# Moving modulation products, convolution steps and the compressed weighing inside the first two layers of a four-engine transformer kernel

## Chip, cores and metric

The kernel runs on one core of one Trainium2 chip, as one program. The metric is device time in microseconds (us), from the first to the last instruction of an execution, as the median of several executions. The engines that matter are PE (TensorE, matmuls), DVE (VectorE), ACT (ScalarE), POOL (GpSimd) and SP (SyncE, which issues the weight loads).

## What is computed

Everything is float32, with 256 tokens of width 1024. Two "first" layers run, and then one "second" block. Cut to what matters:

```python
for l in range(2):                      # the two first layers
    h = rms_norm(x, pre_mix)
    proj = h @ w_in                     # q, kv, gate, conv and pool inputs
    o_a = cmp_attention + selected_attention + window_attention
    o_b = silu(layer_norm(causal_conv31(a * sigmoid(g))))     # 512 channels
    o_c = pool_mixer(...);  o_d = sliding_window_attention(...)
    up = einsum(branches, w_branch);  gates = sigmoid(h @ w_gate)
    x = x + rms_norm(sum(gates * up) @ w_o)
    hf = rms_norm(x, pre_ffn)
    x = x + rms_norm((gelu(gate) * val) @ w_down)   # gate, val: conv3(hf @ w_up)
# second block: it starts from x and from modulation vectors
mods = silu(c) @ w_mod + b_mod          # 6 x 1024, for c and for c_ctx
```

`mods` needs nothing from the first layers. The kernel works it out inside them.

## The kernel before, in words

**Weights.** All weights come in chunks of 128 x 2048 floats (1 MB) through a ring of four slots, `ring`. The chunk with index c of a layer goes to slot c % 4. SP issues the loads strictly in the order of the index, in the loop of line 450, and each load first waits until PE has used the chunk four places ahead of it. A layer has 92 chunks. Most are *split* chunks: ACT rounds the chunk (`split_hi`, L423) into a high part, DVE subtracts (`split_lo`, L428, into `ring_low`), and PE then makes three matmuls for each product. A few chunks are *raw*: PE reads them from the ring. Raw ones are the compression weights, one pad chunk and the modulation halves. The list `layer_chunks()` says which chunk is of which kind, and `SPLIT_CHUNKS[n]` gives the chunk index of split n.

**Modulation.** In each layer there are 6 steps of 512 columns, each in two halves (`mod_half`, L495, one raw chunk, four column groups), then ACT copies the row (`mod_out`), PE turns it (`mod_turn`, L508) and DVE adds the bias (`mod_in`, L1160). Steps 0 to 2 stand among the 16 gate blocks, steps 3 to 5 among the 22 feed-forward blocks.

**Every engine's order is written by hand.** A layer's stages on PE are:

1. `turn_normed("ht")` (L482), then the projections kv, kv2, q, dq, two split chunks each (L547 to L551).
2. Gate inputs, compression, convolution and pool inputs.
3. Seven rounds (r = 0 to 6) of two gate blocks each (L577 to L581), with the attention's scores (L704), the turning of its probabilities (L717) and its values (L734, L740) in between. `cmp_out` turns the compressed probabilities `csc` in round 1. It needs DVE's `cmp_weigh` (L1348 to L1357).
4. Sixteen branch products (`up`, L794 to L798) in the order of branches 2, 0, 3, 1. In front of `up` (0, 3) PE turns the convolution's result `acc` (`convT`, L482), which needs all 124 convolution steps of DVE (`conv_steps`, L1267). Later it turns the normed result (`obT`).
5. The output projection `wo`, four split chunks (L813 to L817), then `turn_normed("hf")` behind two norms, the feed-forward blocks (L835 to L839), and the down projection (L857 to L861).

**DVE in a round:** `mask` twice (wait for PE's scores), `split_lo` for one gate block, `weigh` twice (wait for ACT's exponentials), `split_lo` for the next gate block, then 12 convolution steps. In round 1 `cmp_weigh` comes behind the first `split_lo`.

**ACT behind the output projection.** For each column half c of `wo`, ACT first splits two chunks and then squares the result. For c = 1 these two are the first two chunks of the feed-forward stage (FIRST_WO is 38, FIRST_FFN is 42):

```python
for c in range(2):
    for n in range(FIRST_WO + 2 + 2 * c, FIRST_WO + 4 + 2 * c):
        split_hi(act, n)
    for t in range(TT):
        post_square("wo", c, t)
```

DVE has the same order (`split_lo` of both, then `residual`). At a layer's end ACT calls the next layer's `highs_head` (its splits 0 and 1) and then `post_square("down", 1, t)`; DVE calls `lows_head` and then `residual("down", 7)`. Behind `post_square` come POOL's roots, DVE's residual, and the next norm: ACT's square (L887), POOL's root, DVE's gains (L1141), ACT's scaling (L892), and then PE's `turn_normed`.

Of the kernel before, what the change touches and what calls it, by code (L numbers as in the profile page):

```python
# [27 lines left out]
F32 = mybir.dt.float32  # L28
# [186 lines left out]
def plan_layer(jobs):  # L215
    for t in range(TT):
        for c in range(2):
            jobs.plan(("ht", t, c))
# [40 lines left out]
    for i in range(MOD_STEPS // 2):  # L259
# [18 lines left out]
    for i, r in zip(range(3, MOD_STEPS), ("s0", "s1", "t")):  # L278
# [7 lines left out]
CONV_BEFORE = (0, 3)  # L286
OB_BEFORE = {(3, 1): 0, (3, 2): 1}
# [3 lines left out]
def layer_block(nc, l, mem, ring, ring_low, landed, used, wts, psum, sems, cols_dram, rows_dram, turner_in, placed, wait_x, wait_scratch):  # L291
# [161 lines left out]
    def tensor_program(pe):  # L453
# [32 lines left out]

        def mod_half(i, half):
# [28 lines left out]
        def next_split():  # L516

            n = split_at["n"]
            split_at["n"] += 1
            assert state["chunk"] == SPLIT_CHUNKS[n], (state, n)  # L520
# [11 lines left out]
        pe.wait_ge(turner_in, 16)  # L532
        turn_normed("ht", 1)

        for w in ("kv", "kv2", "q", "dq"):
            for half in range(2):
# [19 lines left out]
                else:  # L556
                    jobs.fill(mm, (w, 1))
                    release(w)

# [264 lines left out]

        turn_normed("hf", 2)
# [47 lines left out]
    def scalar_program(act, next_heads):  # L873
# [178 lines left out]
        for n in range(FIRST_UP + 2, FIRST_UP + 6):  # L1052
            split_hi(act, n)
        for t in range(TT):
            if t == 1:
                split_hi(act, FIRST_UP + 6)
# [8 lines left out]
        for n in range(FIRST_UP + 7, FIRST_WO + 1):  # L1065
# [32 lines left out]
        for j in range(FB + 1):  # L1098
# [13 lines left out]
            if j < FB:  # L1112
                if MOD_AFTER_FFN.get(j - 1, (0, 0))[1] == 1:
                    mod_out(MOD_AFTER_FFN[j - 1][0])
# [14 lines left out]
    def vector_program(dve, next_heads):  # L1129
# [74 lines left out]
        for t in range(TT):  # L1204
            jobs.wait_drained(dve, ("kv", t))
            dve.tensor_copy(kd[:, t, :, :, :], bc(proj[:, t, 0:256].rearrange("p (m d) -> p m d", m=4).unsqueeze(2), [P, 4, 2, DH]))\
               .then_inc(kd_ready, 1)
        split_lo(dve, 4)
# [160 lines left out]
        for r in range(len(ROUNDS) + 1):  # L1369
# [9 lines left out]
            if r == 1:  # L1379
                cmp_weigh()  # L1380
# [10 lines left out]
            conv_steps(12)  # L1391
# [24 lines left out]
        for bi, n in enumerate(BRANCH_ORDER):  # L1416
            dve.wait_ge(gates_ready, bi + 1)
            for i in range(4):
# [15 lines left out]
                if (n, i + 1) == (3, 3):  # L1434
                    for t in range(TT):
                        dve.wait_ge(ob_hi, t + 1)
                        part = brS[1][:, :, :, t * P:(t + 1) * P]
                        dve.tensor_tensor(part[:, 1, :, :], acc[:, :, t * P:(t + 1) * P], part[:, 0, :, :].bitcast(F32),
                                          ALU.subtract).then_inc(ob_lo, 1)
                if i % 2 == 0:  # L1440
                    conv_steps(3)
                else:
                    chunk = 2 * bi + i // 2
                    if chunk < 7:
                        split_lo(dve, FIRST_UP + chunk + 2)
                    conv_steps(5 if chunk < 2 else 4 * TAPS)
# [67 lines left out]
    def gpsimd_program(pool):  # L1514
# [52 lines left out]

        k = 0
        for n in BRANCH_ORDER[1:]:
            for i in range(4):  # L1570
# [6 lines left out]
                if (n, i + 1) == CONV_BEFORE:  # L1577
                    conv_roots()
# [3 lines left out]
        for j in range(FB):  # L1582
            u = hq[j % 2][:, (j // 2 % 2) * 512:(j // 2 % 2) * 512 + 512]
            pool.wait_ge(gelued, j + 1)
            if j:
# [9 lines left out]
                heads=dict(load_pre=load_pre, load_cols=load_cols, highs=highs_head, lows=lows_head), x_ready=x_ready, post_sq=post_sq)  # L1595
# [1304 lines left out]
def build_program(nc, x_in, ctx_in, cond, weights, cols, rows, cols2, rows2, const, out):  # L2900
    with ExitStack() as ctx:
# [15 lines left out]
        with ExitStack() as first:  # L2917
# [27 lines left out]
            for l in range(LAYERS):  # L2945
# [9 lines left out]

                layers.append(layer_block(nc, l, mem1, ring, ring_low, landed, used, weights, psum,
# [203 lines left out]
```

## Time and profile before

| | |
|---|---|
| median of 3 runs | 1823.33 us (1822.49 to 1829.71) |
| profiled execution: its own time, its span | 1830.08 us, 1828.0 us |
| granted TensorE clock, mean | 0.951 of full |
| first layer / second layer / second block | 0 to 547.94, 547.94 to 1090.59, 1090.59 to 1828.0 us |
| PE busy in the three | 506.60, 506.44, 667.47 us |
| DVE busy in the three | 368.35, 365.02, 351.36 us |

The page's shares are means over the span. In both layers PE works almost without a break; its waits there are few, and each comes back in the second layer at the same place. A wait is read from the bracket of a timeline row: it gives the idle time in front of the instruction and what ended it. The clock column (PEclk) of a stretch is 1.00 at 2.4 GHz and 0.50 at 1.2 GHz.

### The profile page before, as it was taken

To read this page: it belongs to the slowest core of one execution; us is meant where nothing else is said; L and a number is where in the kernel's file an instruction comes from. 1 tells how busy PE (TensorE), PEld (TensorE's weight loads), DVE (VectorE), ACT (ScalarE), POOL (GpSimd) and SP (SyncE) were. 2 spreads that over 40 slices of the span, in tenths; PEclk is the share of its full clock that TensorE was granted. 3 is DMA by queue.
4 is the path that set the end of the run, shared out by engine and by line. 5 is a ranking of instruction groups with operands and counts; after the bars stand their busy time and mean duration, and the time that the engine had idled before them with its cause. 6 is when DMAs were issued, how large, how long until landed. Compare 5 with 4: busy or idle time off the path is not lost. (4 is left out here: it accounts for less than half of the span.)

```text
span 1828.0 us, 26603 instructions
## 1 busy us (share of the span) xinstructions
PE 1680.5 (92%) x10712; PEld 1383.9 (76%) x10712; DVE 1084.7 (59%) x1490; ACT 760.2 (42%) x1069; POOL 261.6 (14%) x293
## 2 busy tenths in 40 slices
PE   7998997899998989998899989999898978999996
PEld 5887897699977888887799974445475537899995
DVE  4668987566645668987566631284547334454555
ACT  4355654455534355554455422113116224333431
POOL 0200004144301200003144200014320000000000
PEclk9999998899999999998899999999869987999998
DMA  6544454466553545454466554112000232355551
GB/s 252 185 185 162 185 185 151 149 234 250 184 200 139 211 157 184 169 178 158 151 237 224 187 185 170 69 69 91 25 23 1 70 115 93 139 184 184 184 182 70
DMA packets 40121, 282.07 MB, mean 154 GB/s; under 512 B 4816, under 2 KB 5072, under 8 KB 6864
## 3 DMA queue, kind: packets, MB, share of 16 engines
q1 hardware_dynamic: 38432, 273.15, 41.4%
q10 hardware_dynamic: 1584, 7.42, 1.2%
q8 instruction: 78, 1.28, 0.3%
q14 instruction: 27, 0.22, 0.0%
HBM read 279.50 MB, written 1.05 MB: 153 GB/s over the span
## 5 line engine op out<-in xcount | busy, mean ns | idle before, releaser
L428 DVE TENSOR_TENSOR ring_low<-ring,sb_hi 128x2048 fp32r<-128x2048 f32 x116 | 267.9, 2309 | 192.3 <-ACT sb_hi L423 191.9
L423 ACT ACTIVATE sb_hi<-ring 128x2048 fp32r<-128x2048 f32 x116 | 222.5, 1918 | 285.9 <-DMA ring<-weights 114.4
L577 PE MATMUL psum<-sb_hS,sb_hi 128*128 128x256 f32 x704 | 203.3, 289 | 4.8 <-DVE ring_low L428 4.7
L1848 DVE TENSOR_TENSOR sb_split<-ring,sb_split 128x2048 fp32r<-128x2048 f32 x48 | 109.9, 2292 | 153.2 <-ACT sb_split L1843 153.2
L580 PE MATMUL psum<-sb_hS,sb_hi 128*128 128x256 f32 x704 | 200.3, 284 | 0.0
L581 PE MATMUL psum<-sb_hS,ring_low 128*128 128x256 f32 x704 | 199.4, 283 | 0.0
L839 PE MATMUL psum<-sb_hfT,ring_low 128*128 128x256 f32 x704 | 198.1, 281 | 0.0
L2162 PE MATMUL psum<-sb_hfS,sb_split 128*128 128x256 f32 x512 | 146.5, 286 | 6.0 <-DVE sb_hfS L2692 3.9
L2165 PE MATMUL psum<-sb_hfS,sb_split 128*128 128x256 f32 x512 | 145.8, 285 | 0.0
L2166 PE MATMUL psum<-sb_hfS,sb_split 128*128 128x256 f32 x512 | 145.8, 285 | 0.0
L577 PEld LDWEIGHTS psum<-sb_hS,sb_hi 128*128 128x128 f32 x704 | 134.9, 192 | 14.1 <-DVE ring_low L428 7.2
L581 PEld LDWEIGHTS psum<-sb_hS,ring_low 128*128 128x128 f32 x704 | 136.3, 194 | 0.0
L580 PEld LDWEIGHTS psum<-sb_hS,sb_hi 128*128 128x128 f32 x704 | 134.7, 191 | 0.0
L839 PEld LDWEIGHTS psum<-sb_hfT,ring_low 128*128 128x128 f32 x704 | 134.5, 191 | 0.0
L428 DVE TENSOR_TENSOR ring_low<-ring,sb_hi_ffn 128x2048 fp32r<-128x2048 f32 x34 | 79.7, 2350 | 64.2 <-ACT sb_hi_ffn L423 64.2
L1843 ACT ACTIVATE sb_split<-ring 128x2048 fp32r<-128x2048 f32 x48 | 91.4, 1906 | 54.2 <-PE psum L2130 18.1
L835 PE MATMUL psum<-sb_hfT,sb_hi_ffn 128*128 128x256 f32 x384 | 109.9, 286 | 1.3 <-DVE sb_hfT L1153 1.3
L838 PE MATMUL psum<-sb_hfT,sb_hi_ffn 128*128 128x256 f32 x384 | 109.7, 286 | 0.0
L2162 PEld LDWEIGHTS psum<-sb_hfS,sb_split 128*128 128x128 f32 x512 | 99.3, 194 | 8.3 <-issue 8.0
L1267 DVE SCALAR_TENSOR_TENSOR sb_acc<-sb_bglu,sb_cols,sb_acc 128x256 f32<-128x256 f32 x240 | 101.5, 495 | 0.0
L2165 PEld LDWEIGHTS psum<-sb_hfS,sb_split 128*128 128x128 f32 x512 | 99.3, 194 | 0.3
L2166 PEld LDWEIGHTS psum<-sb_hfS,sb_split 128*128 128x128 f32 x512 | 99.2, 194 | 0.0
(392 smaller groups left out, 3881.7 us busy)
## 6 DMA issues: line engine op xcount, KB each, us to landing
ring<-weights SPq DMA_DIRECT2D x256, 1024.0 KB, 4.8
sb_rows_ffn<-rows ACTq DMA_DIRECT2D x4, 512.0 KB, 4.7
sb_rows_mix<-rows ACTq DMA_DIRECT2D x2, 1024.0 KB, 5.0
sb_rows<-rows ACTq DMA_DIRECT2D x1, 2048.0 KB, 9.1
sb_x<-x_in SPq DMA_DIRECT2D x2, 512.0 KB, 5.9
sb_y<-ctx_in SPq DMA_DIRECT2D x1, 1024.0 KB, 6.4
out<-sb_x SPq DMA_DIRECT2D x2, 512.0 KB, 2.7
sb_const<-const SPq DMA_DIRECT2D x1, 711.0 KB, 13.5
```

Source lines behind the costliest of these rows:

```text
L423: act.activation(hi_of(n), ring[:, c % SLOTS, :], ACT.Copy).then_inc(hi_ready, 1)
L428: eng.tensor_tensor(low_of(n), ring[:, SPLIT_CHUNKS[n] % SLOTS, :], hi_of(n).bitcast(F32), ALU.subtract).then_inc(lo_dve, 1)
L577: mm = pe.matmul(out, hi[:, k, bs], hS[:, 0, k, :], start=(k == 0), stop=False)
L580: pe.matmul(out, hi[:, k, bs], hS[:, 1, k, :], start=False, stop=False)
L581: mm = pe.matmul(out, lo[:, k, bs], hS[:, 0, k, :], start=False, stop=(k == KD - 1))
L835: mm = pe.matmul(out, hi[:, k, b * P:(b + 1) * P], hfT[:, 0, k, :], start=(k == 0), stop=False)
L838: pe.matmul(out, hi[:, k, b * P:(b + 1) * P], hfT[:, 1, k, :], start=False, stop=False)
L839: mm = pe.matmul(out, lo[:, k, b * P:(b + 1) * P], hfT[:, 0, k, :], start=False, stop=(k == KD - 1))
L1848: dve.tensor_tensor(split[:, n % SPLITS, 1, :], ring[:, (first_moe + n) % SLOTS, :], split[:, n % SPLITS, 0, :].bitcast(F32), ALU.subtract ...
L2162: mm = pe.matmul(out, hi[:, k, b * P:(b + 1) * P], hfS[:, 0, k, :], start=(k == 0), stop=False)
L2165: pe.matmul(out, hi[:, k, b * P:(b + 1) * P], hfS[:, 1, k, :], start=False, stop=False)
L2166: mm = pe.matmul(out, lo[:, k, b * P:(b + 1) * P], hfS[:, 0, k, :], start=False, stop=(k == KD - 1))
```

## The change

Chunk indices below are those within a layer. The parts of the change:

- **Head.** The halves (0, 0) and (0, 1) become chunks 1 and 2, between the two chunks of kv; split 1 becomes chunk 3. In layer 1 PE makes them before `turn_normed("ht")`, in layer 0 behind it. `mod_turn(0)` stands behind kv, `mod_out(0)` on ACT behind split 2, `mod_in(0)` on DVE behind the copies of kv.
- **Gates.** The four halves left there stand behind gate blocks 2, 3, 6 and 7, the turns behind 4 and 8.
- **Behind the output projection.** The halves (3, 0), (3, 1), (4, 0), (4, 1) become chunks 53 to 56, between the last chunk of `wo` and the first of the feed-forward stage, which becomes chunk 57. Their turns are behind blocks 3 and 7. Step 5 stays, step 4 and step 5 change regions.
- **Convolution.** Rounds 0 to 6 take 4, 20, 16, 14, 16, 14 and 18 steps in place of 12 each up to 98 with the 14 behind them (116 now). The rest follows `up` (2, 0). `convT` is moved from in front of `up` (0, 3) to in front of `up` (2, 3), that is from the eighth branch product to the fourth; `obT` from (3, 1) and (3, 2) to (0, 2) and (3, 0).
- **Compressed weighing.** In round 1 `cmp_weigh` comes before the first `split_lo`.

```diff
-MOD_AFTER_GATE = {2: (0, 0), 3: (0, 1), 5: (1, 0), 6: (1, 1), 8: (2, 0), 9: (2, 1)}
-TURN_AFTER_GATE = {4: 0, 7: 1, 10: 2}
-MOD_AFTER_FFN = {1: (3, 0), 3: (3, 1), 6: (4, 0), 8: (4, 1), 11: (5, 0), 13: (5, 1)}
-TURN_AFTER_FFN = {5: 3, 10: 4, 15: 5}
+HEAD_MODS = [(0, 0), (0, 1)]
+MOD_AFTER_GATE = {2: (1, 0), 3: (1, 1), 6: (2, 0), 7: (2, 1)}
+TURN_AFTER_GATE = {4: 1, 8: 2}
+MODS_AFTER_WO = [(3, 0), (3, 1), (4, 0), (4, 1)]
+MOD_AFTER_FFN = {11: (5, 0), 13: (5, 1)}
+MOD_OUT_IN_FFN = {1: 3, 3: 4, 14: 5}
+TURN_AFTER_FFN = {3: 3, 7: 4, 15: 5}
...
-    return ["split"] * FIRST_BA + ["raw", "split"] * 4 + gates + ["split"] * 12 + ffn + ["split"] * (FB // 2)
+    return (["split"] + ["raw"] * len(HEAD_MODS) + ["split"] * (FIRST_BA - 1) + ["raw", "split"] * 4 + gates + ["split"] * 12
+            + ["raw"] * len(MODS_AFTER_WO) + ffn + ["split"] * (FB // 2))
...
-CONV_BEFORE = (0, 3)
-OB_BEFORE = {(3, 1): 0, (3, 2): 1}
+CONV_BEFORE = (2, 3)
+OB_BEFORE = {(0, 2): 0, (3, 0): 1}
+CONV_STEPS = (4, 20, 16, 14, 16, 14, 18)
...
+        def head_mods():
+
+            if wait_down is not None:
+                wait_down(pe)
+            for i, half in HEAD_MODS:
+                state["chunk"] = 1 + half
+                mod_half(i, half)
+            state["chunk"] = 0
...
         pe.wait_ge(turner_in, 16)
+        if l > 0:
+            head_mods()
         turn_normed("ht", 1)
+        if l == 0:
+            head_mods()
...
+            if w == "kv":
+                mod_turn(0)
...
+        for i, half in MODS_AFTER_WO:
+            mod_half(i, half)
         turn_normed("hf", 2)
...
             split_hi(act, 2 * i + 2)
+            if i == 0:
+                mod_out(0)
             split_hi(act, 2 * i + 3)
...
+            if r == 1:
+                cmp_weigh()
             split_lo(dve, FIRST_GATE + 2 * r + 1)
...
-            if r == 1:
-                cmp_weigh()
...
-            conv_steps(12)
+            conv_steps(CONV_STEPS[r])
...
                 if i % 2 == 0:
-                    conv_steps(3)
+                    conv_steps(4 * TAPS)
```

`wait_down` waits until DVE has drained ("down", 0, 1) of the layer before. ACT's splits around `obT`, DVE's two subtractions for `ob_lo` and POOL's `conv_roots` are moved along with `obT` and `convT`.

## Rows read from the trace of the kernel before

**Rows 1.** Page, part 1: busy time, share of the span, instructions.
```profile
PE 1680.5 (92%) x10712; PEld 1383.9 (76%) x10712; DVE 1084.7 (59%) x1490; ACT 760.2 (42%) x1069; POOL 261.6 (14%) x293
```
**Rows 2.** PE's waits in both layers: us in total, times, longest.
```profile
PE psum L482 <- ACT sb_tm L892: 32.1, 4, 11.4
PE psum L482 <- DVE sb_acc L1267: 16.5, 2, 8.2
PE psum L482 <- DVE sb_csc L1357: 12.1, 2, 6.0
PE psum L794 <- issue: 2.6, 2, 1.3
```
**Rows 3.** Stretches: length, busy PE, PEld, DVE, ACT, POOL, PEclk, DMA share, GB/s.
```profile
23.74:29.50 5.76, 5.76 (x26) 4.62 (x25) 2.29 (x1) 1.92 (x1) 0.00 (x0) 1.00 0.54 182
144.34:150.00 5.66, 5.66 (x28) 5.66 (x29) 4.54 (x9) 3.16 (x4) 0.00 (x0) 0.53 0.54 185
144.20:221.35 77.15, 76.75 (x606) 66.05 (x606) 66.81 (x114) 42.16 (x98) 0.00 (x0) 0.96 0.50 183
285.08:290.00 4.92, 4.92 (x25) 4.92 (x26) 3.87 (x7) 0.00 (x0) 2.75 (x5) 0.54 0.00 0
346.50:354.50 8.00, 7.34 (x33) 6.98 (x34) 3.52 (x5) 2.39 (x4) 0.12 (x1) 0.50 0.74 262
```
**Rows 4.** DVE's timeline before `csc` is turned in layer 0: start, us.
```profile
134.16 3.25 DVE L1267 SCALAR_TENSOR_TENSOR sb_acc<-sb_bglu,sb_cols,sb_acc 128x256 f32<-128x256 f32 x8
139.96 2.28 DVE L428 TENSOR_TENSOR ring_low<-ring,sb_hi 128x2048 fp32r<-128x2048 f32 x1
```
**Rows 5.** DVE's waits from 144.20 to 221.35.
```profile
DVE sb_proj L1307 <- PE psum L704: 3.7, 1, 3.7
DVE ring_low L428 <- ACT sb_hi L423: 3.5, 2, 2.5
DVE sb_sc L1307 <- PE psum L704: 1.8, 1, 1.8
```
**Rows 6.** Timeline behind the output projection of layer 0.
```profile
332.01 3.97 ACT L423 ACTIVATE sb_hi_ffn<-ring 128x2048 fp32r<-128x2048 f32 x2
...
339.92 0.60 ACT L1083 ACTIVATE sb_acc<-psum 128x512 f32<-128x512 f32 x1 [2.08 <-PE psum L817]
340.00 1.28 DVE L1467 SCALAR_TENSOR_TENSOR sb_x<-sb_tm,sb_small,sb_x 128x1024 f32<-128x1024 f32 x1 [0.50 <-POOL sb_small L1533]
...
341.70 0.55 POOL L1533 TENSOR_TENSOR sb_small<-sb_small,sb_const 128x1 f32<-128x1 f32 x1
...
346.50 3.67 PE L482 MATMUL psum<-sb_const,sb_tm 128*128 128x128 f32 x16 [6.62 <-ACT sb_tm L892]
```
**Rows 7.** Modulation half, load issued behind it, a pair of loads, the split behind.
```profile
153.69 1.06 PE L495 MATMUL psum<-ring,sb_cvec 128*32 128x512 f32 x8
154.91 0.33 SPq L450 DMA_DIRECT2D ring<-weights  x1
365.15 0.86 SPq L450 DMA_DIRECT2D ring<-weights  x2
372.51 1.92 ACT L423 ACTIVATE sb_hi_ffn<-ring 128x2048 fp32r<-128x2048 f32 x1 [4.41 <-DMA ring<-weights]
```
**Rows 8.** Page, part 6: issues, KB each, median us to landing.
```profile
ring<-weights SPq DMA_DIRECT2D x256, 1024.0 KB, 4.8
```
**Rows 9.** Timeline at the boundary of the two layers.
```profile
542.57 5.97 SPq L450 DMA_DIRECT2D ring<-weights  x2
547.98 0.60 ACT L1083 ACTIVATE sb_acc<-psum 128x512 f32<-128x512 f32 x1 [1.66 <-PE psum L861]
549.16 1.28 DVE L1467 SCALAR_TENSOR_TENSOR sb_x<-sb_tm,sb_small,sb_x 128x1024 f32<-128x1024 f32 x1 [0.50 <-POOL sb_small L1533]
555.48 1.73 PE L482 MATMUL psum<-sb_const,sb_tm 128*128 128x128 f32 x7 [7.54 <-ACT sb_tm L892]
```
**Rows 10.** Timeline of layer 0's head, kv2's first split.
```profile
25.77 2.29 DVE L428 TENSOR_TENSOR ring_low<-ring,sb_hi 128x2048 fp32r<-128x2048 f32 x1 [5.79 <-ACT sb_hi L423]
```

More of the change, by code:

```diff
@@ L258, in plan_layer @@
             jobs.plan(("O", a, t), "u", drains=2)
-    for i in range(MOD_STEPS // 2):
+    for i in range(1, MOD_STEPS // 2):
         jobs.plan(("mod", i), "t")
@@ L277, in plan_layer @@
         jobs.plan(("ffn", j))
-    for i, r in zip(range(3, MOD_STEPS), ("s0", "s1", "t")):
+    for i, r in zip(range(3, MOD_STEPS), ("s0", "t", "s1")):
         jobs.plan(("mod", i), r)
@@ L283, in plan_layer, with layer_block @@
             jobs.plan(("down", c, t), ("s0", "s1", "t", "u")[2 * t + c])
-CONV_BEFORE = (0, 3)
-OB_BEFORE = {(3, 1): 0, (3, 2): 1}
+CONV_BEFORE = (2, 3)
+OB_BEFORE = {(0, 2): 0, (3, 0): 1}
+CONV_STEPS = (4, 20, 16, 14, 16, 14, 18)
 BRANCH_ORDER = (2, 0, 3, 1)
-def layer_block(nc, l, mem, ring, ring_low, landed, used, wts, psum, sems, cols_dram, rows_dram, turner_in, placed, wait_x, wait_scratch):
+def layer_block(nc, l, mem, ring, ring_low, landed, used, wts, psum, sems, cols_dram, rows_dram, turner_in, placed, wait_x, wait_scratch, wait_down):
     filled = {r: sems(f"filled_{r}") for r in REGION}
@@ L519, in next_split @@
             split_at["n"] += 1
+            if n == 1:
+                state["chunk"] += len(HEAD_MODS)
             assert state["chunk"] == SPLIT_CHUNKS[n], (state, n)
@@ L1051, in scalar_program @@
         open_gates(BRANCH_ORDER[3], 2)
-        for n in range(FIRST_UP + 2, FIRST_UP + 6):
+        for n in range(FIRST_UP + 2, FIRST_UP + 4):
             split_hi(act, n)
         for t in range(TT):
-            if t == 1:
-                split_hi(act, FIRST_UP + 6)
+            split_hi(act, FIRST_UP + 4 + t)
             jobs.wait_filled(act, ("obT", t))
@@ L1064, in scalar_program @@
         load_rows(act, "post_mix", 2 * D, mem["rows_mix"][:, :, :].rearrange("p i c -> p (i c)"), mix_rows_in)
-        for n in range(FIRST_UP + 7, FIRST_WO + 1):
+        for n in range(FIRST_UP + 6, FIRST_WO + 1):
             split_hi(act, n)
@@ L1433, in vector_program @@
                     conv_norm()
[L1434 to L1439, printed above, removed]
                 if i % 2 == 0:
-                    conv_steps(3)
+                    conv_steps(4 * TAPS)
                 else:
                     chunk = 2 * bi + i // 2
+                    if chunk == 4:
+                        for t in range(TT):
+                            dve.wait_ge(ob_hi, t + 1)
+                            part = brS[1][:, :, :, t * P:(t + 1) * P]
+                            dve.tensor_tensor(part[:, 1, :, :], acc[:, :, t * P:(t + 1) * P], part[:, 0, :, :].bitcast(F32),
+                                              ALU.subtract).then_inc(ob_lo, 1)
                     if chunk < 7:
                         split_lo(dve, FIRST_UP + chunk + 2)
-                    conv_steps(5 if chunk < 2 else 4 * TAPS)
                     if chunk == 6:
@@ L2954, in wait_scratch, with wait_down @@
                         eng.wait_ge(before, 4 * TT)
+                def wait_down(pe, before=layers[-1]["jobs"] if l else None):
+                    before.wait_drained(pe, ("down", 0, 1))
                 layers.append(layer_block(nc, l, mem1, ring, ring_low, landed, used, weights, psum,
-                                          lambda name, l=l: sems(f"{name}_{l}"), cols, rows, turner_in, placed, wait_x, wait_scratch))
+                                          lambda name, l=l: sems(f"{name}_{l}"), cols, rows, turner_in, placed, wait_x, wait_scratch,
+                                          wait_down if l else None))
             heads = [layer["heads"] for layer in layers[1:]] + [None]
@@ L3081, in layer_inputs @@
     down = i["ffn_w_down"][l].reshape(FB, P, 2, 512).transpose(2, 0, 1, 3)
+    kv0 = k_split(kv[:, 0:512])
     chunks = [
-        k_split(kv[:, 0:512]), k_split(np.concatenate([kv[:, 512:768], w[:, 1816:2072]], 1)),
+        kv0[0:1], *[mod[j][half] for j, half in HEAD_MODS], kv0[1:2], k_split(np.concatenate([kv[:, 512:768], w[:, 1816:2072]], 1)),
         k_split(pairs(w[:, 0:512], DH)), k_split(pairs(w[:, 1304:1816], DH)),
@@ L3087, in layer_inputs @@
         *[br[n].reshape(4, P, 2, 512).transpose(2, 1, 0, 3).reshape(2, P, CH) for n in BRANCH_ORDER],
-        k_split(i["w_o"][l][:, 0:512]), k_split(i["w_o"][l][:, 512:1024]), *ffn,
+        k_split(i["w_o"][l][:, 0:512]), k_split(i["w_o"][l][:, 512:1024]),
+        *[mod[j][half] for j, half in MODS_AFTER_WO], *ffn,
         down.reshape(FB // 2, BLOCKS, P, 512).transpose(0, 2, 1, 3).reshape(-1, P, CH),
```

12 lines of the change are left out of this document (7 added, 5 removed).

## The prediction

> **What bounds the kernel now.** I read the page's busy times first [rows 1]: PE is busy for 92% of the span, so time can only come from PE's breaks, from its slow clock, or from nothing. The change touches only the two layers, 0 to 1090.59. Next I read whom PE waits for there [rows 2]. Three kinds of wait hold nearly all of it: the norms in front of `turn_normed` (four times, 32.1 us), the convolution in front of `convT` (8.2 in each layer), and the compressed weighing (6.0 in each). Then the stretches right behind such waits [rows 3]: PE works at 0.50 to 0.54 of its clock, 1.2 in place of 2.4 GHz, for about 5.3 us behind `csc`, 4.6 behind `convT` and 8 behind `hf`. Half of that is lost, so a closed wait gives back 2.7 or 2.3 us more than its length.
>
> PE's work is not changed, only moved: each modulation half takes 1.06 us [rows 7], 1.0 from start to next start. A half gains only where it fills a wait, and the question is what its new place does to the ring.
>
> **The ring, which the change also moves.** A load is issued only when PE has used the chunk four places ahead. Before, the first two feed-forward chunks were loaded in place of the first two `wo` chunks, and ACT had split them at 332.01 to 335.98, before `wo` ended at 339.88 [rows 6]. Now chunks 53 to 56 are modulation halves, so chunk 57 (split 42) waits for half 53 and chunk 58 (split 43) for half 54, and both are used only behind `wo`. ACT and DVE still split 42 and 43 in front of the squares and the residual that `hf` needs. The covered loads lie bare. The same holds at the layer's end: split 1 is now chunk 95 counted from layer 0's start, which waits for the very last chunk of the down projection, and ACT splits it ahead of the last squares.
>
> **Behind the output projection, E = its end.** Half 53 starts at E. A half's start to the load that its release allows took 1.2 us (153.69 to 154.91 [rows 7]), so load 56 goes at E+1.2, 57 at E+2.2, 58 at E+3.2. A load alone lands 4.8 us after its issue [rows 8]: E+6.0 for 56. Of the pair issued from 365.15, the second was awaited until 372.51 [rows 7], that is 7.4 behind the first issue, 2.6 behind the first landing. So 57 lands at about E+8.5 and 58 at E+11.1; a pair in a busier stretch could cost a microsecond more for each. ACT splits 57 at E+8.6, 58 at E+11.1 to 13.0 (two took 3.97 [rows 6]). Then two squares of 0.6 each, until E+14.2. POOL's roots, from the square's end (340.62) to 342.25 [rows 6], take 1.5 us or a little more for each tile: E+15.3 and E+16.8. DVE ends `split_lo` 43 (2.28 [rows 4]) at E+15.3, the gains take 0.7 (estimated as half of a residual), and the first tile's residual (1.28 [rows 6]) ends at E+17.3. From the end of that one (341.28) to `turn_normed` (346.50) took 5.2 us [rows 6]. So `hf` is turned at E+22.5 in place of E+6.6: **+15.9 us per layer**. Four halves lie in it and leave the feed-forward stage, −4.0. The slow 8 us behind `hf` I keep: a wait was there before. Lower bound: if 57 and 58 landed with no queueing, at E+7.0 and E+8.0, their splits would end at E+10.9, 2.1 us less. Upper bound +3 for slower pairs.
>
> A rule can be weighed here. The Trainium skill, "DMA: Bandwidth & Descriptors", section "Anatomy of one DMA — SWDGE (gpsimd) path", fits one transfer as about 2.0 us plus its bytes over 436 GB/s, for another issuing path than this one. That gives an estimate of 4.4 us for 1 MB and 2.4 for each one queued behind, and the chain would end some 0.8 us earlier per layer, a total 1.6 us lower. The trace has 4.8 and 2.6 here, and I go by the trace.
>
> **Layer boundary, E2 = 547.94.** The two issues from 542.57 end at 548.54 [rows 9]; the second, for chunk 95, is at 548.20 and lands 4.8 later, at E2+5.1. Before, nothing waited for it; ACT squared at 547.98 [rows 9]. Now ACT splits it until E2+7.0, squares until E2+8.3, DVE's `split_lo` 1 ends at E2+9.3, gains 0.7, residual 1.28: E2+11.3. Before, the first residual ended at 550.44 and `turn_normed` came 5.04 later [rows 9]. So E2+16.3 in place of E2+7.5: **+8.8**, once. The two halves fill 2.0 of it; their saving is counted in the gates below.
>
> **kv2, both layers.** Split 2 is now chunk 4 and is loaded only when chunk 0 is used, at the end of kv's first half K. Before, chunk and split were ready early: DVE began `split_lo` at 25.77, K+2.0 [rows 10]. Now the load is issued at K+0.2 (as at the boundary, 547.94 to 548.20), lands at K+4.9, and after 1.9 and 2.3 us PE may start at K+9.2. kv's second half ends at K+5.8 (23.74 to 29.50 [rows 3]); the turn of step 0 fills 0.9 of the rest. So kv2 starts 3.5 us late, a little idle time. In layer 0 the halves stand behind `turn_normed` on a PE still at its slow rate and fill only 1.1 us of waiting, so K itself is 1.5 later. Chunk 3 of layer 0 is loaded at the start with the whole ring and needed at 25, so it is hidden. Layer 0: **+5.0**, layer 1: **+3.5**.
>
> **The gate rounds.** Eight convolution steps fewer stand before round 1's masks: 8 × 0.406 = 3.2 us [rows 4]; `cmp_weigh` stands before the 2.2 of `split_lo` that began at 139.96. It ends at 138.9 in place of 144.2; PE was free at 138.3, 6.0 before 144.34. The 6.0 wait nearly goes. But what is late next is DVE. From 144.20 to 221.35, where gate block 11 begins, DVE had 9.0 us of waits in 77.15 [rows 3, 5]. Now it starts 5.3 earlier and has in addition 2.2 (that `split_lo`) and 18 steps (66 in place of 48) × 0.403 = 7.3. That is 9.5 of work into 9.0 of waits, and one wait stays: chunk 32's load follows the half behind gate 6, which costs DVE about 1.1. So gate 11 starts 5.3 + 9.0 − 9.5 − 1.1 = **3.7 us earlier**, and no more, although PE lost a 6.0 wait, 2.7 of slow clock and 3.0 of modulation (two halves, one turn). New waits of PE for `ring_low`, 1 to 3 us in front of gates 5, 7, 9 and 11, take the rest. Bounds: 2.5, if any handover slips; 13 if DVE kept up everywhere.
>
> **The branch products.** The last 8 steps (3.2 us) follow `up` (2, 0). PE makes (2, 1) and (2, 2) meanwhile, 5.7 us, so `convT` comes just in time: DVE has drained (2, 0) some 2.2 us into (2, 1), and ends 0.2 before PE. I went through the silus behind `obT` and the subtractions for `ob_lo` in the same way: each ends before PE asks for it, the nearest, for branch 1, by 0.2 us. So the 8.2, the 2.3 of clock and the 1.3 in front of branch 1 [rows 2] go: **−11.7 per layer**. Lower bound −9, if `convT` waits 2.5 us.
>
> **Sum.** Layer 0: +5.0 − 3.7 − 11.7 + 15.9 − 4.0 = +1.5. Layer 1: +8.8 + 3.5 − 3.7 − 11.7 + 15.9 − 4.0 = +8.8. Together **+10.3 us**: the profiled execution would go from 1830.1 (span 1828.0) to about 1840. It lay 6.7 above the median, and I add to the median: 1823.3 + 10.3 = **1833.6**, or 0.57% slower. Within 0.5% (9.1 us) is what a measurement of this kernel can tell from no change.
>
> **The rivals.**
> 1. *The loads stay hidden* (ends on the other side). If splits 42, 43 and the next layer's 1 were ready as before, the 15.9 twice and the 8.8 go: 1833.6 − 40.6 = 1793. For it: every other load of the stage is hidden. Against: the rule of four places. It decides where the delay behind `wo` falls below 6.2 us per layer, which needs split 43 ready at E+3.3, while its load is issued at E+3.2.
> 2. *DVE keeps up in the rounds.* PE then gains its wait, clock, modulation and the small waits it had, 13 us per layer in place of 3.7: 1815. For it: DVE's mean share is 59% [rows 1]. Against: in the stretch that counts it is 87% busy [rows 3] and is given 9.5 us more. Half of it gives 1824.
> 3. *More waits than I count.* Loads in pairs slower by a microsecond each, `convT` not ready (2.5 per layer), a slow clock behind the new waits of 3 us (1.7 each): 1843.
>
> **Chances.** My forecast (1826 to 1840) 0.55, rival 1 0.06, rival 2 in full or half 0.17, rival 3 0.19, no effect 0.03. Slower by over 0.5%: 0.38 of mine and rival 3, 0.57. Within: 0.17 of mine, 0.09 of rival 2, 0.03: 0.29. Faster: 0.06 and 0.08 of rival 2: 0.14. The range from 1815 to 1844 leaves out rival 1 and the tail of rival 3.
>
> **What would show it.** In the profile after: ACT's split 42 ended by a load some 8 us behind `wo`; about 16 us between the halves and `hf`'s turning; a split that waits for its load at 553, with the squares behind it; PE waiting 3 us for kv2's `ring_low`; no wait of PE at `convT`; DVE without waits from 139 to 216, and PE waiting for `ring_low` in front of gates 5, 7, 9 and 11. I am wrong if `hf` is turned under 15 us behind `wo`, or if PE does not wait in the rounds.

## The result, and the profile after

The changed kernel takes **1850.55 us** (median of 4 runs, 1844.90 to 1854.31) where the kernel before takes 1826.52 in the same session: ratio **1.0129**, 95% interval 1.009 to 1.0168. It is 24.0 us slower. I had forecast 10.3 us slower, 1833.6 in a range from 1815 to 1844: the direction was right, and the time lies outside the range. One execution of experiment e3 below took 2973.8 us at a granted clock of 0.73; it stands in no time and no ratio here.

The page of the changed kernel, part 1, beside [rows 1]: PE, DVE and ACT have the same work, and the instructions are as many on every engine.

```profile
PE 1680.9 (91%) x10712; PEld 1382.2 (75%) x10712; DVE 1085.4 (59%) x1490; ACT 760.7 (41%) x1069; POOL 243.9 (13%) x293
```

Whom PE waits for in both layers (us in total, times, longest), beside [rows 2]:

```profile
PE psum L489 <- ACT sb_tm L918: 56.7, 4, 15.4
PE psum L601 <- DVE ring_low L435: 21.9, 11, 3.0
PE psum L511 <- DMA ring<-weights: 6.6, 2, 3.3
PE psum L524 <- ACT sb_mrow L927: 4.2, 2, 2.1
...
PE psum L489 <- DVE sb_csc L1385: 1.3, 2, 0.7
```

The wait for `acc` (16.5) is gone and the one for `csc` nearly (12.1 before, 1.3 now). In their place the norms take 24.6 more, the low parts of gate blocks come up eleven times (four times and 4.7 us before), and two kinds of wait are new: a half for its own load (L511), and the turn of step 0 for its row (L524).

Where the time went, stage by stage. Each number is the time from the first matmul of one stage to the first of the next, read from PE's groups by line; "forecast" is what my sum holds for it.

| stage (layer 0 / layer 1) | before | after | difference | forecast |
|---|---|---|---|---|
| start, or last matmul of layer 0, to kv | 16.1 / 11.5 | 17.8 / 20.5 | +1.7 / +9.0 | in the next / +8.8 |
| kv to the first scores | 97.1 / 96.5 | 102.8 / 105.4 | +5.7 / +8.9 | +5.0 (start included) / +3.5 |
| scores to branch products | 143.6 / 143.9 | 141.8 / 143.2 | −1.8 / −0.7 | −3.7 / −3.7 |
| branch products to `wo` | 59.4 / 59.6 | 48.1 / 48.0 | −11.3 / −11.6 | −11.7 / −11.7 |
| `wo` to the first feed-forward block | 34.6 / 34.6 | 50.5 / 50.5 | +15.9 / +15.9 | +15.9 / +15.9 |
| feed-forward to down | 136.0 / 136.0 | 131.4 / 131.5 | −4.6 / −4.5 | −4.0 / −4.0 |

Down itself takes 60.5 us in both, within 0.1. The rows add up to +5.6 and +17.0; the second block adds 1.7, and that is the 24.3 by which the spans differ (1828.0 to 1852.3). The profiled executions lie 3.6 and 3.8 us above their kernels' medians, so the two differences can be compared. The forecast holds in four of the six rows. It fails in two: from kv to the scores (2.4 and 5.4 too little) and in the rounds, from the scores to the branch products (1.9 and 3.0 too much gain).

**Behind the output projection** it went as worked out. ACT, then DVE, then PE of layer 0, timeline rows (start, length, what ended the idle time before), beside [rows 6]:

```profile
342.63 1.91 ACT L430 ACTIVATE sb_hi_ffn<-ring 128x2048 fp32r<-128x2048 f32 x1 [16.25 <-DMA ring<-weights]
345.11 1.91 ACT L430 ACTIVATE sb_hi_ffn<-ring 128x2048 fp32r<-128x2048 f32 x1 [0.58 <-DMA ring<-weights]
346.93 0.57 ACT L1110 ACTIVATE sb_acc<-psum 128x512 f32<-128x512 f32 x1
...
350.44 1.29 DVE L1494 SCALAR_TENSOR_TENSOR sb_x<-sb_tm,sb_small,sb_x 128x1024 f32<-128x1024 f32 x1 [0.49 <-POOL sb_small L1560]
...
334.07 2.78 PE L511 MATMUL psum<-ring,sb_cvec 128*32 128x512 f32 x24
340.15 1.06 PE L511 MATMUL psum<-ring,sb_cvec 128*32 128x512 f32 x8 [3.31 <-DMA ring<-weights]
356.67 2.18 PE L489 MATMUL psum<-sb_const,sb_tm 128*128 128x128 f32 x9 [15.45 <-ACT sb_tm L918]
```

E, the end of the output projection, is 334.1. The two loads land at E+8.5 and E+11.0 (forecast 8.5 and 11.1), the first square stands behind both splits at 346.93, and `hf` is turned at E+22.6, where the prediction said 22.5. The fourth half waits 3.31 us for its load, inside a wait that was there anyhow.

**At the boundary** of the layers it is the same: split 1 starts 5.0 us behind the end of the down projection (553.6; forecast 5.1) and the norm is turned 16.6 behind it (forecast 16.3). ACT and PE, beside [rows 9]:

```profile
558.61 1.91 ACT L430 ACTIVATE sb_hi<-ring 128x2048 fp32r<-128x2048 f32 x1 [10.00 <-DMA ring<-weights]
560.43 0.58 ACT L1110 ACTIVATE sb_acc<-psum 128x512 f32<-128x512 f32 x1
...
570.17 1.54 PE L489 MATMUL psum<-sb_const,sb_tm 128*128 128x128 f32 x6 [14.35 <-ACT sb_tm L918]
```

**Behind kv, layer 1.** PE stands still in front of the turn of step 0: ACT copies the row only when it has made the late split 2 (from 584.35; the copy starts at 586.16). What runs behind is at half clock: the turn takes 1.66 us where it takes 1.02 in layer 0, the first matmul of kv2 0.79 where it takes 0.50 there.

```profile
584.39 0.40 PE L573 MATMUL psum<-sb_hi,sb_hS 128*128 128x512 f32 x1
586.89 1.66 PE L524 MATMUL psum<-sb_const,sb_mrow 128*128 128x2 f32 x8 [2.10 <-ACT sb_mrow L927]
588.63 0.79 PE L569 MATMUL psum<-sb_hi,sb_hS 128*128 128x512 f32 x1
```

The whole stage from kv to the scores, layer 0 and layer 1 (length, busy PE, PEld, DVE, ACT, POOL, granted clock, DMA share, GB/s), before and then after:

```profile
16.10:113.20 97.10, 93.40 (x626) 79.53 (x627) 56.32 (x69) 40.11 (x42) 11.05 (x17) 1.00 0.57 208
558.80:655.30 96.50, 92.98 (x628) 79.91 (x626) 53.92 (x67) 39.39 (x43) 11.04 (x17) 0.98 0.52 190
```

```profile
17.80:120.60 102.80, 96.02 (x640) 81.82 (x636) 54.91 (x67) 41.12 (x43) 11.04 (x17) 0.97 0.57 210
573.50:678.90 105.40, 98.61 (x638) 84.24 (x636) 54.01 (x68) 39.92 (x44) 11.04 (x17) 0.94 0.53 195
```

The start of kv2 (29.14 and 570.20 before, 33.12 and 588.63 after) cuts this stage in two. From kv's start to kv2's start layer 1 takes 3.8 us more (forecast 3.5). Layer 0 is 4.0 later there with its start (forecast 5.0): kv starts 1.7 later but runs its first half in 5.7 us in place of 7.4, its early matmuls taking 0.40 us each where they took 0.63, so the 1.5 that I had added for it did not come. Up to kv2 the forecast is right or too high. What it lacks lies behind kv2's start, where it has nothing and where 3.4 and 5.2 us were lost. The same columns from kv2's start to the scores, before and then after:

```profile
29.14:113.20 84.06, 80.39 (x579) 69.08 (x578) 50.15 (x64) 36.81 (x40) 11.05 (x17) 1.00 0.57 206
570.20:655.30 85.10, 81.58 (x579) 70.61 (x577) 50.24 (x64) 36.76 (x40) 11.04 (x17) 0.98 0.56 203
```

```profile
33.12:120.60 87.48, 83.58 (x580) 71.90 (x580) 50.33 (x65) 35.38 (x40) 11.04 (x17) 0.96 0.54 197
588.63:678.90 90.27, 85.66 (x580) 73.76 (x580) 50.33 (x65) 35.48 (x40) 11.04 (x17) 0.93 0.52 192
```

Over the whole stage, PE's idle time (length less busy) in layer 1 grows from 3.5 to 6.8 us, by 3.3. The other 5.6 of the 8.9 is PE being busy longer, with ten more instructions (eight of them the turn). The clock column tells why: at 0.94 the stage loses 6% of 105.4 us, 6.3, and at 0.98 it lost 1.9. These 4.4 us I had not counted. In layer 0 the clock column falls from 1.00 to 0.97, worth 3.1. Not all of it stands behind kv2's break: in layer 0 half of it lies behind the first gate block's wait (2.28 us at 102.34, 2.09 before), which was there in the kernel before too, but at full clock behind. One trace is not the measure of it: the changed head stands in e2, e4, e6 and e12 as well, where this stage takes 102.4 to 103.4 us in layer 0 and 102.7 to 104.6 in layer 1, and the old head in e1, e3 and e8, where it takes 94.9 to 96.3 and 95.1 to 96.9. The miss is there in each of them.

**In the rounds** DVE no longer waits for PE from 139 on. It waits twice for a split that waits for its load, once for chunk 32, which I had counted at 1.1, and once for chunk 26, which I had not (ACT and DVE, layer 0; then all of DVE's waits from 144.62 to 227.06, beside [rows 5]):

```profile
150.78 1.92 ACT L430 ACTIVATE sb_hi<-ring 128x2048 fp32r<-128x2048 f32 x1 [3.57 <-DMA ring<-weights]
...
152.74 2.29 DVE L435 TENSOR_TENSOR ring_low<-ring,sb_hi 128x2048 fp32r<-128x2048 f32 x1 [2.21 <-ACT sb_hi L430]
```

```profile
DVE ring_low L435 <- ACT sb_hi L430: 3.6, 2, 2.2
```

Chunk 26 belongs to gate block 4 and is loaded when gate block 2's chunk is released. In the kernel before, the load of gate block 4 ran from 138.5 to 143.3, inside the 6 us that PE waited for `csc`, and DVE waited only 1.0 us for the split. With that wait gone, the load is late. e3, which closes the wait and leaves all halves where they were, has the same wait of DVE there, 2.11 us.

### The profile page after: what moved, and what is told of

It is laid out like the page before. It is cut to its first block and busy times, and to the rows that moved or that the text cites. A ratio compares the mean times of both kernels' runs of the same rounds, so it can differ in the third digit from the quotient of the medians.

```text
span 1852.3 us, 26601 instructions
## 1 busy us (share of the span) xinstructions
PE 1680.9 (91%) x10712; PEld 1382.2 (75%) x10712; DVE 1085.4 (59%) x1490; ACT 760.7 (41%) x1069; POOL 243.9 (13%) x293
## 5 line engine op out<-in xcount | busy, mean ns | idle before, releaser
L1521 DVE SCALAR_TENSOR_TENSOR sb_hq<-psum,sb_cols,sb_hq 128x254 f32<-128x254 f32 (+1 forms) x176 | 72.6, 475 | 45.5 <-ACT sb_hq L1133 45.5
```

## The experiments

Times are medians of 3 to 10 executions; "against after" takes 1850.6, measured in another session than any of these. The executions of one kernel lie up to 9.4 us apart, so a difference of medians below some 5 us says little by itself, and I read the small ones from the traces. The kernel before stood at 1828.5, 1828.4 and 1828.7 in the three sessions.

| | kernel | us | ratio to before (95%) | against after |
|---|---|---|---|---|
| e1 | behind-`wo` part alone | 1849.4 | 1.0129 (1.0097 to 1.0162) | −1 |
| e2 | head part alone | 1850.5 | 1.0121 (1.0091 to 1.0151) | 0 |
| e3 | rounds, convolution, weighing alone | 1808.0 | 0.9896 (0.9862 to 0.9929) | −43 |
| e4 | after, splits behind the norms | 1822.7 | 0.9976 (0.9962 to 0.9991) | −28 |
| e5 | after, head's chunk order | 1837.7 | 1.0050 (1.0034 to 1.0067) | −13 |
| e6 | after, halves spread over the gates | 1841.1 | 1.0062 (1.0045 to 1.0079) | −10 |
| e7 | after, extra matmuls behind the turn | 1856.2 | 1.0143 (1.0123 to 1.0163) | +6 |
| e8 | e3 and two halves behind `wo` | 1803.9 | 0.9864 (0.9842 to 0.9886) | −47 |
| e9 | after with e4, e5 and e6 | 1798.5 | 0.9832 (0.9817 to 0.9847) | −52 |
| e10 | e8 with the head, e5 and e6, split 1 behind the parts of `ht` | 1793.2 | 0.9805 (0.9788 to 0.9821) | −57 |
| e11 | after, extra matmuls around the turn | 1844.7 | 1.0081 (1.0065 to 1.0096) | −6 |
| e12 | after, 24 steps fewer in the rounds | 1861.5 | 1.0182 (1.0167 to 1.0198) | +11 |

### The three parts alone (e1, e2, e3)

Each is the kernel before with one part of the change (of each diff the lines that set it). e1:

```diff
+MODS_AFTER_WO = [(3, 0), (3, 1), (4, 0), (4, 1)]
+MOD_AFTER_FFN = {11: (5, 0), 13: (5, 1)}
```

> Only the halves behind the output projection and the feed-forward turns; head, gates and convolution as before. Theory A (covered loads lie bare, ACT and DVE split feed-forward chunks 42 and 43 in front of the squares): 15.9 us later at the turning of hf in each layer, 4.2 given back in the feed-forward stage, so about +23 us, ratio 1.013; the wait in front of hf reads 15.5 us. Rival B (the loss of the whole change lies in the gate rounds and the head, this part gains as the halves fill a wait of 6.6): -8 us, ratio 0.996.

e2:

```diff
+HEAD_MODS = [(0, 0), (0, 1)]
+MOD_AFTER_GATE = {2: (1, 0), 3: (1, 1), 6: (2, 0), 7: (2, 1)}
```

> Only the halves at the layer's head (and the gates without them). Theory A: +8.8 at the boundary, +3.7 at kv2 in each layer, -3.0 in each layer's gates, +10 without any clock effect. Theory C (the slow clock falls behind new waits of 2 to 3 us at kv2 and costs what the sum missed): 7 to 9 us more, +17 to +19, ratio 1.010, with stretches at PEclk 0.5 behind kv2 in both layers. Rival: no clock stretches there, +10, ratio 1.005.

e3:

```diff
+CONV_BEFORE = (2, 3)
+OB_BEFORE = {(0, 2): 0, (3, 0): 1}
+CONV_STEPS = (4, 20, 16, 14, 16, 14, 18)
...
+            if r == 1:
+                cmp_weigh()
```

> Only the convolution steps, the places of convT and obT and the earlier weighing; all modulation halves where they were. Theory A: 11.5 us per layer from convT, and only about 2 from the rounds, since DVE has no waits left there: -26 us, ratio 0.986. Rival B (the new waits for ring_low in the rounds eat the gain): over -10, ratio above 0.994. If DVE kept up: -38.

Measured: +20.8 (23 expected), +22.0 and −20.5 us, together +22.3 where the whole change costs 24.0. So the change is one gain of 20 and two losses of 21 and 22. The head (e2) cost twice the 10 us expected without the clock, and more than the 17 to 19 with it. The stage from kv to the scores is 5.4 and 7.9 us longer (3.7 expected in each layer), and the gates without its two halves are only 0.4 us shorter in each layer, where I had expected 3.0. The rounds (e3) gave less than I expected of them, and the kernel 20.5 in place of 26. They are 144.7 and 144.9 us long (143.6 and 143.9 before): the `csc` wait closed and nothing came of it. The whole gain is the convolution's: from the branch products to `wo` it takes 48.0 us in layer 0 (59.4 before).

### Splits behind the norms (e4)

On both engines the splits of chunks 57 and 58 stand behind the parts of `hf`, and the next layer's split 1 behind the parts of `ht` (the lines for `hf`):

```diff
         high_parts("hf", hfT)
-        split_hi(act, FIRST_FFN + 2)
+        for n in range(FIRST_FFN, FIRST_FFN + 3):
+            split_hi(act, n)
...
         low_parts("hf", 1, hfT)
-        split_lo(dve, FIRST_FFN + 2)
+        for n in range(FIRST_FFN, FIRST_FFN + 3):
+            split_lo(dve, n)
```

> The changed kernel, but ACT and DVE split chunks 42 and 43 behind the turned hf parts and the next layer's split 1 behind the ht parts, so that squares, residual and norms go first. Theory A: PE turns hf 6.6 us behind wo again and waits about 15 us in all until block 0 (26.8 in the changed kernel), -11.6 per layer, and -8.8 at the boundary: -32 against the changed kernel, about 1818, ratio to before 0.996. Rival (the loads themselves are too late, whatever the order): within 5 us of the changed kernel.

PE of layer 0 and then of the boundary, e4:

```profile
339.28 1.07 PE L509 MATMUL psum<-ring,sb_cvec 128*32 128x512 f32 x8 [3.24 <-DMA ring<-weights]
348.49 0.58 PE L859 MATMUL psum<-sb_hfT,sb_hi_ffn 128*128 128x256 f32 x1 [4.81 <-DVE ring_low L435]
...
547.58 1.09 PE L487 MATMUL psum<-sb_const,sb_tm 128*128 128x128 f32 x8 [3.56 <-ACT sb_tm L916]
```

The wait of 15.45 is gone: `hf` is turned at 340.28, 7.0 us behind the end of `wo` (expected 6.6). What is late next is the first block's own low part, 4.81. From `wo` to the first block took 38.8 and 40.1 us in place of 50.5, and from the last matmul of layer 0 to kv 9.5 in place of 20.5, less than before the change (11.5), since the halves stand in the wait and split 1 behind it. The loads were as late as in the changed kernel; only what stood behind them on the two engines was taken away. The medians fall by 27.9 and the profiled executions by 31.3, where 32 was expected. Of what the change lost, the splits and squares behind bare loads were the largest part.

### The head's chunk order (e5)

```diff
-    return (["split"] + ["raw"] * len(HEAD_MODS) + ["split"] * (FIRST_BA - 1) + ["raw", "split"] * 4 + gates + ["split"] * 12
+    return (["raw", "split"] * 2 + ["split"] * (FIRST_BA - 2) + ["raw", "split"] * 4 + gates + ["split"] * 12
```

with the weights, the slots that PE names and the order of the first four loads to match.

> The changed kernel with one difference: the first four chunks of a layer stand in the order half, kv, half, kv in place of kv, half, half, kv, so kv2's first chunk is loaded behind a half, which is used early, and no longer behind kv's first chunk. Theory A (the part of the loss that I had not forecast is mostly slow clock behind new breaks of PE of 2 to 3 us): PE's breaks in front of kv2 go (3.7 us in layer 0, about 3 in layer 1), and with them the half-clock stretches behind them (3.4 us in layer 0, 6.8 in layer 1, half of each lost), so 10 to 12 us less than the changed kernel, ratio to before about 1.006 to 1.007. Rival B (only the waits count): 6 to 7 us less, ratio about 1.009, with the half-clock stretches still there. The late split at the layers' boundary stays in both.

The stage from kv to the scores, layers 0 and 1, e5:

```profile
17.20:115.30 98.10, 94.19 (x640) 80.69 (x636) 55.35 (x68) 41.16 (x43) 11.04 (x17) 0.98 0.60 222
569.10:665.10 96.00, 92.21 (x638) 79.06 (x636) 53.91 (x69) 40.04 (x44) 11.07 (x17) 1.00 0.56 203
```

4.7 and 9.4 us shorter than after. PE's idle time falls by 2.9 and 3.0 us; in layer 1 the clock column goes from 0.94 to 1.00 as well, worth 6.3 of the other 6.4. Part of the gain was given back in the rounds (144.5 and 144.4 us in place of 141.8 and 143.2). The median fell by 12.9, theory A's 10 to 12 and a little more.

### Extra matmuls in the wait (e7, e11)

```diff
             if w == "kv":
-                mod_turn(0)
+                jobs.claim(pe, ("kv2", 0))
+                for n_fill in (9, 3):
+                    for _ in range(n_fill):
+                        pe.matmul(jobs.out(("kv2", 0)), hS[:, 0, 0, 0:P], hS[:, 0, 0:2, :], start=True, stop=False, skip_group_check=True)
+                    if n_fill == 9:
+                        mod_turn(0)
```

This is e11; e7 has all 12 behind `mod_turn(0)`. Both add work whose result is overwritten, and nothing else.

> The changed kernel with 12 extra matmuls of 512 columns on PE (about 2.8 us, their result is overwritten) in front of kv2, where PE otherwise waits for kv2's split. No wait is removed, the time at which kv2 can start stays. Theory A (the clock falls because PE stood still): the half-clock stretches behind kv2 (3.4 us from 34.1, 6.8 from 587.1) go, and the kernel gets 3 to 5 us faster than the changed one, ratio about 1.010. Rival B (the clock has another cause there): no change, 1.013, or slower by what the extra matmuls run over the end of the wait.

> The changed kernel with 12 extra matmuls of 512 columns on PE, nine in front of the turn of step 0 (2.1 us, where PE waits 2.1 us) and three behind it (0.7 us, where it waits 0.8 us for kv2's split); their result is overwritten. In the earlier run with all of them behind the turn PE still stood still for 1.8 us ahead of them and the clock fell. Theory A (the clock falls because PE stood still): no half-clock stretch behind 29 us and behind 584 us, scores of layer 1 some 3 us earlier, 3 to 5 us less than the changed kernel in all. Rival B: the stretches stay, no gain.

e7 could not tell the theories apart: I had put the matmuls behind the turn, and PE stood still in front of it for 1.81 and 2.16 us, about as before. The twelve then ran in large part at half clock, took 4.59 and 5.40 us and ended behind the wait, so kv2 started later. e11 mends that: its twelve take 3.2. The ten microseconds from the end of kv in layer 1, after and then e11:

```profile
584.20:594.20 10.00, 7.82 (x25) 6.12 (x24) 5.33 (x5) 5.28 (x5) 0.00 (x0) 0.66 0.73 288
```

```profile
583.20:593.20 10.00, 10.00 (x47) 7.79 (x46) 5.33 (x5) 5.29 (x5) 0.00 (x0) 1.00 0.71 288
```

PE has some 3 us more to do in each layer and no load and no split comes earlier: kv2 starts 15.2 us behind kv in layer 1 and 15.3 in layer 0, as in the changed kernel. Behind it, up to the scores, layer 1 takes 83.7 us in place of 90.3 at a clock of 1.00 in place of 0.93, and layer 0 85.6 in place of 87.5 at 0.98 in place of 0.96. The whole stage falls from 105.4 to 98.9 and from 102.8 to 100.9. By the medians the kernel is 5.9 us faster than the changed one, with ratios to before whose intervals just overlap (1.0065 to 1.0096 and 1.0090 to 1.0168), and part of the gain is given back in the rounds (143.2 and 145.9 us). The break of 2.10 us in layer 1 cost more through the clock (0.66 in the ten microseconds shown, 3.4 lost) than by its length.

### The halves in the gates (e6)

```diff
-MOD_AFTER_GATE = {2: (1, 0), 3: (1, 1), 6: (2, 0), 7: (2, 1)}
-TURN_AFTER_GATE = {4: 1, 8: 2}
+MOD_AFTER_GATE = {2: (1, 0), 5: (1, 1), 7: (2, 0), 9: (2, 1)}
+TURN_AFTER_GATE = {6: 1, 10: 2}
```

> The changed kernel with one difference: the four halves in the gate blocks stand behind gates 2, 5, 7 and 9 in place of 2, 3, 6 and 7, turns behind 6 and 10. Theory (DVE's waits of 2.2 and 1.4 us in the rounds come from loads that two halves close together make late, and DVE sets the pace there): both waits go, and the branch products start 3 to 4 us earlier in each layer, 6 to 8 us in all; ratio to before about 1.009. Rival (DVE's waits are only shifted to other places, or PE's later waits take the gain back): less than 2 us, ratio 1.012 to 1.013.

DVE's waits from 139 to 227, e6: its 3.6 us for late splits have become

```profile
DVE sb_sc L1335 <- PE psum L728: 1.0, 1, 1.0
```

and PE's waits for gate blocks' low parts from 120 to 265 fall from 8.5 to 4.5. The rounds take 139.1 and 139.0 us in place of 141.8 and 143.2. They take 139.0 in both layers of e9 and e10 too, which have the halves in these places, and 141.7 to 146.0 in the five kernels with the changed kernel's places and convolution steps (after, e4, e5, e7, e11). The theory holds. With four slots, PE uses three chunks between the one that frees a slot and the one loaded into it. For gate block 4's chunk these were a half, gate block 3 and a half; with the halves apart there are two gate blocks and one half, and the load has a gate block's time more. With the halves apart the rounds do gain, 4.5 and 4.9 us against before. That is 6.9 of the 10.7 us between the two profiled executions (9.5 between the medians); the rest stands in stages that e6 does not touch.

### DVE's work in the rounds (e12)

```diff
-CONV_STEPS = (4, 20, 16, 14, 16, 14, 18)
+CONV_STEPS = (4, 14, 12, 12, 12, 12, 12)
```

> The changed kernel with 4, 14, 12, 12, 12, 12, 12 convolution steps in the rounds (24 fewer), so that 32 stand behind the first branch product in place of 8: 9.7 us of DVE's work per layer moved behind PE's last need of a gate block's low part. Theory (DVE sets the pace in the rounds as well as at the convolution's end, so its work as a sum counts): the branch products start 6 to 8 us earlier, PE's waits for low parts in the rounds nearly go, and PE waits about as long at the turning of the convolution; the total within 5 us of the changed kernel, above it by the slow clock behind the longer wait. Rival (PE's waits in the rounds are for loads, not for DVE's work): the branch products start where they did, and the 9.7 us stand bare: 19 us slower.

PE's waits from 120 to 320, e12:

```profile
PE psum L489 <- DVE sb_acc L1295: 9.3, 1, 9.3
PE psum L601 <- DVE ring_low L435: 3.6, 4, 1.5
```

The rounds got 4.7 and 6.0 us shorter, so DVE's work was what PE waited for there. But the wait at the convolution is 9.3, and the median is 10.9 above the changed kernel: between the theory's 5 and the rival's 19. DVE could not use the time: its waits for splits grew (3.6 to 5.0 in the rounds, 6.6 to 10.6 behind them, layer 0). And PE ran at half clock from 270.6 to 280.8 behind the long wait. DVE's work is not free to move: what was taken out of the rounds came back in part only.

### Putting it together (e8, e9, e10)

e8 is e3 with two halves, and only two, behind `wo`, in the order half, first block, half, second block; the first block's chunk keeps its distance to `wo`, and only the second one's split moves behind the parts of `hf`.

```diff
-MODS_AFTER_WO = [(3, 0), (3, 1), (4, 0), (4, 1)]
-        *[mod[j][half] for j, half in MODS_AFTER_WO], *ffn,
+MODS_AFTER_WO = [(3, 0), (3, 1)]
+        mod[3][0], ffn[0], mod[3][1], ffn[1], *ffn[2:],
```

> The kernel with the convolution and weighing part alone (1808.0 before, ratio 0.990) plus two modulation halves behind the output projection in the order half, first feed-forward chunk, half, second feed-forward chunk; the first feed-forward chunk keeps its place in the ring and its split, the split of the second moves behind the parts of hf. Theory (filling a wait with halves gains if no load that hf or the first blocks need comes late): the norm chain ends as in the kernel before, the two halves fill the wait, 2 us per layer, 1804, ratio 0.988. Rival (the second chunk's split comes late for block 1, or the other splits are pushed behind it): the gain is given back, 1808 or more.

1803.9: 4.1 less than e3, twice two halves, as worked out. The traces say the same: the stage from `wo` is no longer than before (34.4 us), and the feed-forward stage is 2.2 and 2.3 us shorter than e3's.

> The changed kernel with all three mends together: squares and residual ahead of the splits behind the output projection and at the boundary (alone 28 us less than the changed kernel), the head's chunk order half, kv, half, kv (alone 13 less in the medians), and the halves behind gates 2, 5, 7 and 9 (alone 9.5 less). Theory (three separate late loads, each with the slow clock behind it): they add, less some overlap at the boundary and in the rounds, where DVE sets the pace: about 1803 to 1808, ratio 0.988. Rival (the rounds take the head's gain back, as the times of the branch products in the kernel with the head's order alone hint: 5.3 us early at the scores, 2.6 at the branch products): 1812.

e9 came to 1798.5, 4.5 us below the theory's range: together the mends gave 52, singly 28, 13 and 9.5, so within the scatter they add in full.

> The fastest kernel so far (1803.9: convolution and weighing part, two halves behind the output projection) with step 0 at the head in the order half, kv, half, kv, split 1 behind the parts of ht, and the halves of steps 1 and 2 behind gates 2, 5, 7 and 9. Worked out from the stages of the other runs: layer 0 3.8 later at the scores, 5.7 less from there to the branch products; layer 1 2.0 less at the boundary, 0.7 less to the scores, 5.2 less to the branch products: 9 to 10 less in all, 1794 to 1796, ratio 0.982. Rival (the rounds are bound by DVE and the boundary's gain is lost to a slow clock): 1800 or more.

e10 came to 1793.2, the fastest, just below the 1794 to 1796 expected. PE of the two norm waits in e10, behind `wo` and at the boundary, beside [rows 6] (6.62) and [rows 9] (7.54):

```profile
332.63 3.15 PE L487 MATMUL psum<-sb_const,sb_tm 128*128 128x128 f32 x16 [4.38 <-ACT sb_tm L921]
...
538.58 3.34 PE L487 MATMUL psum<-sb_const,sb_tm 128*128 128x128 f32 x16 [5.23 <-ACT sb_tm L921]
```

The halves stand in the waits, and each wait is shorter by about what two halves take (2.2 and 2.3 us). The three ideas of the change work, at a ratio of 0.9805, once no load that they need is made late by them (PE still waits 14.5 us in all for the gate blocks' low parts).

## Why the prediction was right and wrong

- **The bare loads, right.** +15.9 twice and +8.8: measured +15.9, +15.9 and +9.0. e4 shows the mechanism: it changes only the order of the splits, and 27.9 us go. By the estimate from the Trainium skill ("DMA: Bandwidth & Descriptors", section "Anatomy of one DMA — SWDGE (gpsimd) path") the chain would have ended 0.8 us earlier per layer. The trace disagrees for these loads, which SP issues: they landed at E+8.5 and E+11.0, as worked out from the kernel's own rows, and `hf` was turned at E+22.6.
- **The branch products, right.** −11.7 twice, measured −11.3 and −11.6, with no wait at `convT`.
- **The feed-forward stage, right:** −4.0 forecast, −4.6 and −4.5 measured.
- **kv2: "+5.0" and "+3.5", the step that failed most.** The delay of kv2's start was about right: 4.0 and 3.8 us. The turn fills part of it as I wrote, though in front of it PE stands still for 2.1 us, since its row is copied behind the late split. The failed step is the price: I put the break into the sum at its length and the slow clock behind it at nothing. I knew the price of slow clock from [rows 3] and put it into rival 3 alone, at 1.7 for each. Measured, behind kv2's start 3.4 and 5.2 us more were lost up to the scores, mostly by the clock (0.96 and 0.93 in place of 1.00 and 0.98), so the stage was 8.9 longer in layer 1 and 7.4 longer with its start in layer 0. e11 fills the break and gets 6.5 and 1.9 back; e5 removes it and gets 9.4 and 4.7 back. About 1.7 us of layer 0's loss stands behind the first gate block's wait, where the clock fell this time and not before; neither e5 nor e11 takes that away, and why it fell is open.
- **The gates: "3.7 us earlier", the second step that failed, off by a load.** I let one wait stay for DVE, chunk 32's, 1.1 (it was 1.4), and took DVE's other waits as time to fill. Chunk 26's load, which now costs DVE 2.2 us, had landed inside the `csc` wait that the change closes: I asked what is late next on DVE and not in the ring. With it the stage gave 1.8 and 0.7. e6 brings 4.5 and 4.9. The rule that DVE's pace binds held, but e12 bounds it: of 9.7 us of DVE's work taken out, 4.7 and 6.0 came back.
- **The rivals.** Rival 1 did not come, since the rule of four places holds. Rival 2 did not either: PE waits in front of the gate blocks as said (0.89 to 2.79 us each in the rounds of layer 0). Rival 3 is what happened, though not by its parts: the pairs of loads were not slower and `convT` was ready; the slow clock and one more load made up its sum, and more. Of the signs that I named, two did not come: PE did not wait 3 us for kv2's low part (it waited 2.1 for the turn's row, and 0.8 for the low part in layer 0 only), and DVE did wait in the rounds, 3.6 us.
- **The misses as a sum:** 2.4 and 5.4 at kv2, 1.9 and 3.0 in the rounds, −0.2 and −0.2 in the rest, 1.7 in the second block, where the change does nothing: 14.0, the difference of 24.3 and 10.3. How much of the 1.7 is chance is open; before's own medians in the sessions lie 2.2 apart.

## What to carry to other kernels

In a ring with fixed order, a load has as much time as PE spends on the chunks between the one that frees the slot and the one that is loaded, here three. A short product among these three shortens it: when one is moved to fill a wait, look first at which of the next three loads come late by it, and what stands behind their consumers on each engine. Spread such chunks out, and put what the critical chain needs (here squares and residuals) ahead of anything that can wait for a load. Price a break of a busy PE at its length and again for the clock, and when a wait is closed, ask which load had been landing inside it.

## What the hardware showed that I had not expected

Breaks of the same length are not followed by the same clock. The first gate block waits 2.0 to 3.2 us for its low part in the traces of before, after, e5 and e10, and a later block 2.79 us in two of them; the length of the first matmul behind it tells the clock. Before, layer 0; after, layer 0 (twice); e5, layer 0:

```profile
96.50 0.38 PE L577 MATMUL psum<-sb_hS,sb_hi 128*128 128x256 f32 x1 [2.09 <-DVE ring_low L428]
```

```profile
102.34 0.57 PE L601 MATMUL psum<-sb_hS,sb_hi 128*128 128x256 f32 x1 [2.28 <-DVE ring_low L435]
...
169.03 0.39 PE L601 MATMUL psum<-sb_hS,sb_hi 128*128 128x256 f32 x1 [2.79 <-DVE ring_low L435]
```

```profile
163.82 0.58 PE L601 MATMUL psum<-sb_hS,sb_hi 128*128 128x256 f32 x1 [2.79 <-DVE ring_low L435]
```

The break of 2.79 us is followed by full clock in one kernel and by half clock in the other (granted 0.54 from 163.30 to 170.10 in e5, 1.00 from 166.50 to 172.50 after); one of 2.28 by half clock, one of 2.09 by full. Behind the break of 2.28 the granted clock is 0.51 from 102.30 to 105.80. So a break of 2 to 3 us has, beside its length, a price between nothing and about 3.4 us (half of the 6.8 in e5), and a forecast can only carry a mean of it. What decides between the two no run here shows. The Trainium skill, "TensorE: Matmul & The Clock Gate", section "Why this matters for your kernels", warns of idle gaps of PE and names a length above all of these. The trace disagrees with taking shorter ones for safe, with half clock behind breaks of 2.10 and 2.28 us.
